# Dilated prompt heads by residue mod 4, diagonal tiles only, and the first blocks' row work in another order

## What is computed

```python
DSA_PAIRS = ((128, 1), (512, 4), (2048, 16))       # window, dilation; 2 heads each
def dsa_group_prompt(q, k, v, bias_tab, win, dil):
    '''Query t reads t - dil*j, j = 0..win/dil. ...'''
    ...
    s = jnp.where(valid[None, :, None, None], s + bias, -jnp.inf)
    p, lse = softmax_lse(s)
    o = jnp.einsum('bnrhqk,bnkrhd->bnqrhd', p, vv)...
    return o, lse
def dsa_combine(outs, lses):
    alpha = jax.nn.softmax(jnp.stack(lses, axis=0), axis=0)
    return jnp.concatenate([o * alpha[g][..., None] for g, o in enumerate(outs)], axis=2)
```

## Time and profile before

| | |
|---|---|
| median of 3 runs | 1014.61 us (1014.31 to 1015.29) |
| the profiled execution | 1012.51 us, span 1010.6 us |
| PE busy | 985.0 us, 97% of the span, 7695 matmul records |
| DVE busy | 495.5 us, 49% |
| ACT busy | 339.9 us, 34% |
| POOL busy | 67.3 us, 7% |
| share of PE on the chain that ended last | 90% |
| granted TensorE clock over the span | 0.998 |

### The profile page before, as it was taken

How to read it: one execution, slowest core, us unless ns; L and a number is a source line. 1 busy time by engine, 2 the same in 40 slices (tenths; PEclk the granted TensorE clock), 3 DMA queues, 4 the chain that set the end, 5 groups by cost and what they waited for, 6 DMA issues and landing times.

```text
span 1010.6 us, 18503 instructions
## 1 busy us (share of the span) xinstructions
PE 985.0 (97%) x7695; PEld 956.8 (95%) x7695; DVE 495.5 (49%) x906; ACT 339.9 (34%) x567; POOL 67.3 (7%) x91
## 2 busy tenths in 40 slices
PE   5899999999999999999999999999999999999997
PEld 5799989998998889899999999999999999999997
DVE  5634556655687313353535555554455544333232
ACT  6334233443455342322222343222222222322122
POOL 0100113011100200020204000000000000000000
PEclk9999999999999999999999999999999999999999
DMA  7586336332021564422331223222222223222202
GB/s 247 149 278 182 70 119 123 124 97 74 24 85 42 149 180 147 125 84 85 95 101 55 89 100 105 84 84 85 84 84 84 84 92 99 93 74 74 96 21 89
DMA packets 104605, 104.98 MB, mean 104 GB/s; under 512 B 10766, under 2 KB 101320, under 8 KB 104188
## 3 DMA queue, kind: packets, MB, share of 16 engines
q1 hardware_dynamic: 101224, 92.78, 30.2%
q0 software_dynamic: 3248, 11.03, 3.5%
q10 hardware_dynamic: 52, 0.01, 0.0%
HBM read 97.98 MB, written 14.89 MB: 112 GB/s over the span
## 4 chain that ended last, share of the span: by engine, by line
PE 90%; DVE 4%; DMA 1%; issue 1%; POOL 1%; ACT 1%; SPq 1%; ACTq 0%; DVEq 0%; POOLq 0%
PE acc L440 75%; PE acc L936 3%; PE acc L916 2%; PE acc L999 2%; PE acc L1035 1%; PE acc L926 1%; POOL mt L763 1%; PE acc L982 1%; PE acc L844 1%; PE acc L833 1%; SPq L641 1%; DVE h_lo L1883 1%; PE acc L804 1%; DMA ring<-in_cache_dsa_kv 1%; DVE w_lo L424 0%
## 5 line engine op out<-in xcount | busy, mean ns | idle before, releaser
L440 PE MATMUL acc<-h_hi,w_hi 128*128 128x256 f32 (+1 forms) x1520 | 471.7, 310 | 6.8 <-DVE w_lo L424 3.6
L440 PE MATMUL acc<-h_lo,w_hi 128*128 128x256 f32 (+1 forms) x1520 | 438.1, 288 | 0.0
L440 PE MATMUL acc<-h_hi,w_lo 128*128 128x256 f32 (+1 forms) x1520 | 436.7, 287 | 0.0
L440 PEld LDWEIGHTS acc<-h_hi,w_hi 128*128 128x128 f32 x1520 | 286.5, 188 | 16.7 <-issue 8.5
L440 PEld LDWEIGHTS acc<-h_lo,w_hi 128*128 128x128 f32 x1520 | 286.8, 189 | 6.5 <-issue 3.4
L419 ACT ACTIVATE w_hi<-raw 128x1024 fp32r<-128x1024 f32 x135 | 141.4, 1047 | 437.3 <-PE acc L440 437.2
L440 PEld LDWEIGHTS acc<-h_hi,w_lo 128*128 128x128 f32 x1520 | 286.7, 189 | 0.0
L424 DVE TENSOR_TENSOR w_lo<-raw,w_hi 128x1024 fp32r<-128x1024 f32 x135 | 165.4, 1225 | 111.4 <-ACT w_hi L419 106.8
L440 PE MATMUL acc<-s_hi,w_hi 128*128 128x256 f32 (+1 forms) x352 | 101.6, 288 | 0.0
L440 PE MATMUL acc<-s_lo,w_hi 128*128 128x256 f32 (+1 forms) x352 | 101.3, 288 | 0.0
L440 PE MATMUL acc<-s_hi,w_lo 128*128 128x256 f32 (+1 forms) x352 | 100.7, 286 | 0.0
(11 more groups left out here) (299 smaller groups left out, 1146.3 us busy)
## 6 DMA issues: line engine op xcount, KB each, us to landing
raw<-in_w_in SPq DMA_DIRECT2D x25, 1024.0 KB, 5.5
raw<-in_w_gate_up SPq DMA_DIRECT2D x22, 1024.0 KB, 4.9
raw<-in_w_down SPq DMA_DIRECT2D x8, 1024.0 KB, 5.3
ring<-in_cache_dsa_kv SPq DMA_DIRECT2D x4, 1024.0 KB, 6.8
raw<-in_w_out SPq DMA_DIRECT2D x4, 1024.0 KB, 5.6
out<-in_cache_dsa_kv SPq DMA_DIRECT2D x2, 2016.0 KB
rev<-tab POOLq DMA_DIRECT2D x1, 3840.0 KB, 15.9
ring<-in_cache_moba_k SPq DMA_DIRECT2D x48, 64.0 KB, 2.3
```

The lines of the kernel that those rows point to most:

```text
L440: ins = nc.tensor.matmul(acc[:, bank, 0:HALF[half]], a[:, k, :], two(b[:, kx + k, :], half), start=first and k == k0 and c == 0, stop=last ...
```

## The change

The prompt tokens of the far heads' q, k and v are stored in the order of their residue mod 4 when they leave PSUM, so that a query block of 128 positions holds one residue and needs just the one key tile with the same residue. A unit is now either near (`u` even: the near heads of both j) or far (`u` odd: four far heads, one tile each), still 8 units, one per block from block 18. Near and far parts have their own maxima and sums (`stat`), the probabilities are not normalised before the transposes, and at the end `factors` brings the parts to one softmax: the statistics are transposed on PE, stored to HBM and read back in both orders by POOL's DMAs, made into factors by DVE and ACT, sent through HBM again to all partitions, and DVE multiplies the outputs. Where branch B is handed on (`y_made`) the far heads are read back in their old order with a stride. In the first blocks `split_lo(1)` comes before `x_kept(6)` and `x_kept(7)`, and the row work is spread over blocks 1 to 4 and its PE part goes to block 5. SP's transfers beside (`gd`, `G`, the cache copies) move to later times with it.

```diff
+        def strided(ap):
+            return ap.rearrange("p (a j) -> p j a", a=NT)
+        def far(name, i):
+            return name in ("qb", "kb", "vb") and i > 0
+        ND = 2 * NT
+        units = [(i, [h]) for i in range(NT) for j in range(2) for h in range(6 + j, HEADS, 2)]
...
+        T_SA, T_F = 33, 29.55
...
+            t = t[:, n, 0:T if n < 2 else TP]
+            return t.rearrange("p (j a) -> p j a", a=NT) if n in (3, 4) else t
+        def y_made(n):
+            return strided(qT[:, n, 0:TP]) if n in (3, 4) else y_part(qT, n)
...
@@ SP
-                    yield 3.3
+                    yield 4.3
                     sp.wait_ge(sem("rows_done"), 1)
-                    yield 4
+                    yield 5
-                        yield 4 + g
+                        yield 6 + g
...
@@ POOL
+                def factors():
+                    pool.wait_ge(sem("st_ev"), 1)
+                    pool.dma_start(X["st"].rearrange("o (r p) -> (o r) p", p=P), st_T[:, :]).then_inc(sem("f_moved"), 16)
+                    pool.wait_ge(sem("f_moved"), 16)
+                    for s in range(2):
...
+                    pool.wait_ge(sem("f_dve"), 2)
+                    pool.dma_start(X["F"].rearrange("o (k r t) -> (o r) k t", k=2, t=P), F_exp[:, :, :]).then_inc(sem("f_moved"), 16)
+                    pool.wait_ge(sem("f_moved"), 16 * 8)
...
-                pool.wait_ge(sem("s_used"), ND * 3)
+                factors()
+                pool.wait_ge(sem("f_dve"), 4)
                 set_to(Qpad[:, :, :, :], 0.0, "qpad")
...
@@ PE
-                    yield 1.5
+                    yield 1.3
...
-                    yield 3.45
+                    yield 5.3
                     pe.wait_ge(sem("rows_done"), 2)
...
+                def dilated():
+                    for u in range(ND + 1):
...
+                            for j in range(2):
+                                if near(u):
+                                    ins = nc.tensor.matmul(out[:, j, :], zp[:, j, c:c + P], kT[:, 2, P * (i + 1 - keys_of(u)):P * (i + 1)],
+                                                           start=True, stop=True)
+                                else:
+                                    for g in range(2):
+                                        ins = nc.tensor.matmul(out[:, j, P * g:P * (g + 1)], zp[:, j, c + P * g:c + P * (g + 1)],
+                                                               kT[:, 3 + g, P * i:P * (i + 1)], start=True, stop=True)
...
@@ DVE
+                        if far(name, i):
+                            n = 2 * P
+                            if half == 1:
+                                v.then(scaled(dst[:, TP:T], src[:, n:n + TS], r[:, n:n + TS]))
+                            dst = strided(dst[:, 0:TP])[:, n // NT * half:n // NT * (half + 1), :]
+                            scaled(dst, src[:, 0:n].rearrange("p (j a) -> p j a", a=NT),
+                                   r[:, 0:n].rearrange("p (j a) -> p j a", a=NT)).then_inc(acc_ev, 1)
...
                 def factors():
...
+                    yield T_F
+                    dve.wait_ge(sem("f_moved"), 16 * 7)
...
+                    yield T_F + 0.6
+                    dve.wait_ge(sem("st_ev"), 2)
...
+                    yield T_F + 2.55
+                    dve.wait_ge(sem("f_moved"), 16 * 10)
...
                 x_lo(1)
+                split_lo(dve, 1)
                 x_kept(6)
                 x_kept(7)
```

More of the change, by code:

```diff
@@ L534, in unit_time, with near, keys_of, pair_view @@
         def unit_time(u, part):
[L536 removed]
+            return T_BLK + (u + part) / 4
         def scores_in(u):
[L540 removed]
+            return Sc[:, (ND + u) % 5, 0:widths[u]]
         def bias_of(h, c0, w):
[L543 removed]
+            return TTc[:, h - 6, c0:c0 + w]
+        def near(u):
+            return u % 2 == 0
+        def keys_of(u):
+            return min(u // 2, 1) + 1 if near(u) else 2
+        def pair_view(t, u):
+            w = P * keys_of(u)
+            return t.rearrange("p (j n) -> p j n", j=2)[:, :, 0:w]
+        def stat_of(s, u):
+            return stat[:, s, u % 2, :, u // 2]
         NC4 = (1, 2, 2, 2, 2, 2)
@@ L1067, in _ @@
                 x_turned(3, range(KD))
-                side = Side(rstd_rows(), bias_rows(), turn(), mlstm(), attention(), sample(), sample_outputs(), second_norm())
+                side = Side(rstd_rows(), bias_rows(), turn(), mlstm(), dilated(), attention(), sample(), sample_outputs(), second_norm())
                 def first_tile(half, k):
@@ L1223, in exps, with dilated, queries_of @@
                                          accum_out=dn[:, u % 4:u % 4 + 1]).then_inc(sem("e_done"), 1)
+                def dilated():
+                    def queries_of(u):
+                        act.wait_ge(sem("a_s"), HA * NT)
+                        if u == 0:
+                            act.wait_ge(acc_ev, sum_at[12])
+                        if u >= 2:
+                            act.wait_ge(sem("s_mm"), u - 1)
+                        i, c = u // 2, 2 * P * (u % 2)
+                        for j in range(2):
+                            p = HD * j
+                            if near(u):
+                                ins = nc.scalar.copy(zp[p:p + HD, j, c:c + P], qT[p:p + HD, 2, P * i:P * (i + 1)])
+                            else:
+                                ins = nc.scalar.copy(zp[p:p + HD, j, c:c + 2 * P].rearrange("p (g n) -> p g n", g=2),
+                                                     qT[p:p + HD, 3:5, P * i:P * (i + 1)])
+                            ins.then_inc(sem("zp_in"), 1)
+                    yield T_DIL - 0.3
+                    queries_of(0)
+                    for u in range(ND + 1):
+                        if u >= 1:
+                            yield T_DIL + u + 9 / 16
+                            act.wait_ge(sem("pt_tr"), u)
+                            if u >= 3:
+                                act.wait_ge(sem("o_mm"), u - 2)
+                            w = 2 * P * keys_of(u - 1)
+                            nc.scalar.copy(PTs[:, (u - 1) % 2, 0:w], acc[:, 6, 0:w]).then_inc(sem("pt_ev"), 1)
+                        if u < ND:
+                            yield T_DIL + u + 10 / 16
+                            act.wait_ge(sem("m_done"), u + 1)
+                            view = pair_view(Sc[:, u % 5, :], u)
+                            for j in range(2):
+                                nc.scalar.activation(view[:, j, :], view[:, j, :], ACT.Exp, bias=stat_of(0, u)[:, j:j + 1],
+                                                     accum_out=stat_of(1, u)[:, j:j + 1]).then_inc(sem("e_done"), 1)
+                        if u + 1 < ND:
+                            yield T_DIL + u + 13 / 16
+                            queries_of(u + 1)
+                    yield T_DIL + ND + 15 / 16
+                    act.wait_ge(sem("st_tr"), 1)
+                    nc.scalar.copy(st_T[:, :], acc[0:32, 6, 0:P]).then_inc(sem("st_ev"), 1)
+                    yield T_F + 0.4
+                    act.wait_ge(sem("f_dve"), 1)
+                    nc.scalar.activation(F_exp[:, :, :], F_exp[:, :, :], ACT.Exp).then_inc(sem("st_ev"), 1)
@@ L1388, in _ @@
                 x_hi(1)
-                side = Side(rstd_rows(), turn(), mlstm(), attention(), gates(), sample(), sample_softmax(), merge(), feed())
+                side = Side(rstd_rows(), turn(), mlstm(), dilated(), attention(), gates(), sample(), sample_softmax(), merge(), feed())
                 for w in range(n_all):
```

351 lines of the change are left out of this document (211 added, 140 removed).

## The result

The changed kernel takes 1000.6 us (median of four runs, 999.4 to 1002.8) against 1014.5 before: a ratio of 0.987, 95% interval 0.985 to 0.988. Forecast were 996.0 us and a range of 992.5 to 1000.5. The profiled execution took 1001.37 us, its span is 999.6.

A forecast was written before the change was run, and what follows sets the result against it. PE was taken to bound the kernel. Tiles removed (13.3 us) and first blocks reordered (5.3 us) summed to 18.6 us, taking 1014.6 to 996.0 us at chance 0.70; range 992.5 to 1000.5 us.

The forecast's parts named there:

- What bounds the kernel: Whole kernel: PE, busy 985.0 of 1010.6 us; a change pays where it takes work from PE or ends its waits.
- Term 1: Blocks 18 to 26: 24 dilated tiles removed, each with score, transpose and output; net 13.3 us, bounds 12.5 and 14.1.
- Term 2: First blocks: the new order ends PE's waits and the slow clock before block 3; net 5.3 us, bounds 3.5 and 6.4.
- The new waits: First blocks: second sum of block 2 read late, 0.2 us; turn of ka in block 4 waits, 0.9 us.
- Rival A: First blocks exchange one wait for another, 3 us or more, slow clock behind; only 1.9 us stay: 999.4 us, chance 0.12.
- (a): SP's transfers: `gd` about 1 us later, G wanted at block 7's start with 2 us margin; costed at nothing.
- (b): `factors` near block 29: DMAs land with 4 us margin, DVE's own 4 us fit its spare time; costed at nothing.
- D: DVE stands in `factors` until POOL's DMAs land, PE behind it; a loss of 20 us: 1016 us, chance 0.02.
- (c): Handing on of branch B: three pieces take 1.56 us on DVE, two now strided; costed at nothing.
- rival B: Strided elements double an operation; sums hide it, handing on of branch B loses up to 2.1 us: 998.1 us, chance 0.10.
- C: Dilated units bound by the round trip, PE waiting 0.9 us in each of 8; 7 us lost: 1003 us, chance 0.05.

The follow-up runs named there:

- e5: The changed kernel without the five small DVE operations of the second piece of `factors` and without the two multiplications by the factors: 995.5 us.
- e10: The changed kernel with the second piece of `factors`, its five operations together, moved three rows later: 1001.8 us.
- e9: The changed kernel itself, run again unchanged beside other experiments on one chip: 1000.5 us.
- e7: The changed kernel with the far heads handed on by residue, not turned back, so those rows reach the wrong tokens: 1000.4 us.
- e8: The changed kernel, same results, with DVE's `factors` work cut into seven pieces from block 28 and far factors stored by residue: 997.8 us.
- e11: e8 with POOL's clearing of `Qpad` also put behind the last scores: 997.7 us.
- e13: e11 with the pieces of `factors` whole again (2.4 and 2.05 us), in the same early blocks: 998.5 us.
- e6: The changed kernel with POOL's clearing of `Qpad` moved behind the wait for the last scores: 1000.6 us.
- e14: e11 with POOL's broadcast of the bias rows held until G has landed, and its wait put behind the state stores: 997.5 us.
- e1: The kernel before with only the new order of the first blocks: 1009.5 us, against 1013.9 for the kernel before on that chip.
- e12: e11 with each of the seven pieces of `factors` three units later: 997.2 us.

## Why the prediction was right or wrong

- **What bounds the kernel: right.** e5 shows it: take the waits away and the tiles' time comes out in full.
- **Term 1: right in kind, 0.6 us too small.** 13.9 us by PE's starts (14.4 by `w_lo` from 17 to 29), against 13.3 and a best bound of 14.1. (The bound was added up wrong: half of the 0.8 us of waits was in the 13.3 already, so with all of them gone it is 13.7, and the low end of the range 992.9.) The prices of a score, transposes and outputs stand unchanged in the chain after:

```profile
201.56 0.86 PE acc L986 x4
...
204.63 0.44 PE acc L1002 x4
...
207.48 0.89 PE acc L1014 x8
```

  Block 26's second sum starts at 244.39, 74.3 us behind block 17's (170.12); I had forecast about 74.8. So all of the 0.8 us of small waits went, where I had counted on half. What the table shows beyond it up to `w_lo` 29 is for the most part the late `w_lo` of the kernel before.
- **Term 2: 4.2 in the first profile and e10's, 4.8 to 6.0 in the others, against 5.3.** Some 1.7 us of it is the clock before, which was low from 40 to 50 us, where I had 1.3. Block 3 needs no wait; it starts at 37.11 in e9, where I had 37.2 (38.34 in the first profile):

```profile
36.46 1.23 DVE L435 TENSOR_TENSOR w_lo<-raw,w_hi 128x1024 fp32r<-128x1024 f32 x1 [2.86 <-ACT w_hi L430]
...
41.66 0.40 PE L451 MATMUL acc<-h_hi,w_hi 128*128 128x288 f32 x1 [0.33 <-DVE qT L1572]
...
47.48 0.66 PE L868 MATMUL acc<-con,kT 128*128 128x128 f32 x4 [0.58 <-DVE kT L1571]
```

  The new waits are the two that I had named, 0.3 and 0.6 us for 0.2 and 0.9. Rival A is refuted. What the first profile lacks is one run's: see the last section.
- **(a) SP and G at nothing: a small miss.** "its margin is 2 us" took G's landing from the kernel before, where the broadcast was issued 8 us ahead of G. After, three small DMAs of POOL and their landing (one before) move the broadcast back, and G goes out with it. The timelines of POOL and SP before, then after:

```profile
43.46 0.58 POOL L705 DMA_DIRECT2D rev<-tab  x1 [1.78 <-DMA tab<-tab]
...
51.56 0.35 SPq L608 DMA_DIRECT2D G<-gd  x1
```
```profile
47.55 0.55 POOL L748 DMA_DIRECT2D rev<-tab  x1 [3.89 <-DMA tab<-tab]
...
48.44 0.34 SPq L648 DMA_DIRECT2D G<-gd  x1
```

  Depending on the run that costs nothing or, as `w_lo` shows in e7, e8, e10, e11 and e13, 0.6 to 1.7 us.
- **(b) `factors` at nothing: the step that failed.** The DMA half of it held. They landed in time and DVE never waited for them, which refutes D. But "DVE's own 4 us lie in a stretch where it is busy for 52.48 of 66.20 us" took idle time for cover. Before, from `w_lo` 29 to 34, DVE's idle times there are mostly under 1 us, the longest 1.58, between a maximum, an exponential and a sum, each in order behind the other; 2.45 or 2.7 us in one go fit into none. The work was also sized too small: its three pieces are 5.9 us, not 4. Measured, the second and third piece cost 5.3 us (e5). Not all of that is their own length: of the changed kernel's loss 1.1 us goes away when only POOL's clearing moves (e6), another thing that I had at nothing, so the two overlap. This step makes the miss: without it the gain is 18.75 us; in the first profile term 1 was 0.6 us too small and term 2 1.1 too large, which by luck nearly cancel.
- **(c) strided accesses at nothing: wrong by 0.8 us**, the mechanism of rival B, at 0.8 instead of 2.1. Its sign, sums over 0.42 us, is there too (groups by shape; busy time and mean ns; before, then after, where by the mean four of the eight have strides; the last row is one of them):

```profile
L1438 DVE TENSOR_TENSOR kT<-acc,rstd 128x256 f32<-128x256 f32 x6 | 2.5, 413 | 0.0
```
```profile
L1572 DVE TENSOR_TENSOR kT<-acc,rstd 128x256 f32<-128x256 f32 x8 | 4.1, 511 | 2.0 <-PE acc L451 2.0
...
134.63 0.61 DVE L1572 TENSOR_TENSOR kT<-acc,rstd 128x256 f32<-128x256 f32 x1
```

  A strided sum takes 0.61, a plain one 0.41; PE's next user comes late enough to hide it. L1926 takes 2.04 us for 1024 elements, where e8's plain ones take 0.68 for 512: 1.5 times as long. The rule of the Trainium skill, "SBUF — State Buffer", "Door 1: The DMA port swizzle", that a cross to a new line of 16 bytes pays a penalty, thus speaks of a cost that these rows bear out; the Trainium skill gives no size, and the rows have half as much again where rival B had twice. L1926 reads its factors with a step of exactly 4 values, so that step is not free here either; the sums write with a step of 128.
- **C: refuted where I put it** (no wait for PTs from 174 to 245 us), but it is what happened in the MoBA units once DVE was late.

By the first profile: 14.4 + 4.2 - 6.0 - 0.8 + 0.4 (small waits in the sample part that went) = 12.2, with the 0.5 us of the late `w_lo` 29 in both the first and the third number.

## What to carry to other kernels

A share of busy time says how much work fits, not what size of piece. Before costing an addition at nothing on an engine that is 80% busy, look for its longest idle time there and for who stands in order behind it; then cut the addition to that size. (In these profiles cut pieces in earlier blocks lost 1.9 us instead of 6.0; what the size and the place each did is not separated.) And when a change moves the issue of a transfer, check which large one now goes out beside it.

## What the runs showed of the hardware

**After the same idle time the clock falls in one execution and not in another.** My term 2 counted the low clock behind the idle time before block 3 as a cost that the change ends. There it did end: all 14 profiles with the new first blocks show 1.00 from 30 to 50 us. But other places have it in some executions. In e8 and e14 PE stands still at the same place of the sample part, at 411 to 413 and 410 to 412 us; windows of e8, then of e14:

```profile
411.00:413.00 2.00, 0.41 (x3) 0.34 (x3) 2.00 (x5) 1.35 (x3) 0.00 (x0) 1.00 0.00 0
413.00:415.00 2.00, 2.00 (x11) 2.00 (x10) 2.00 (x4) 0.30 (x1) 0.00 (x0) 0.50 0.00 0
```
```profile
410.00:412.00 2.00, 0.42 (x5) 0.21 (x3) 2.00 (x5) 1.35 (x3) 0.00 (x0) 1.00 0.00 0
412.00:414.00 2.00, 2.00 (x16) 2.00 (x17) 2.00 (x4) 0.59 (x1) 0.00 (x0) 1.00 0.00 0
```

Behind the same wait of 1.58 us for a sum of DVE, with the same matmuls around it, the granted clock falls to 1.2 GHz in one and stays at 2.4 in the other. The two kernels differ in POOL's clearing and broadcast; what decides it, no run shows. In the table a fall cost 1.5 us (e6, e8 and e11, from 40 on) to about 1.6 us (e1, before 40, less its longer wait). Another place for it is at 980 to 995 us, in most profiles; e12's has none at all and gains 15.0 us in the span. The spread of the runs of one kernel, some 4 us, fits with this: the kernel before, beside e1, took 1014.2 to 1016.0 us in runs with a clock of 0.995 over the span and 1012.3 to 1014.0 with 0.998.

**The first products can run at about half speed where the window shows a full granted clock.** After, then e9, the same matmuls:

```profile
17.78 0.41 PE L451 MATMUL acc<-h_hi,w_hi 128*128 128x256 f32 x1
18.42 0.41 PE L451 MATMUL acc<-h_hi,w_hi 128*128 128x256 f32 x1
```
```profile
17.45 0.28 PE L451 MATMUL acc<-h_hi,w_hi 128*128 128x256 f32 x1
17.81 0.28 PE L451 MATMUL acc<-h_hi,w_hi 128*128 128x256 f32 x1
```

Three products take 0.64 us in the one, until 19.5 us, and 0.36 in the other, while both windows show 1.00, here after:

```profile
17.00:19.00 2.00, 2.00 (x11) 2.00 (x11) 2.00 (x6) 2.00 (x7) 0.00 (x0) 1.00 1.09 382
```

A step of 0.21 us is also what products of this shape take in e8 at 414 us, in the window with the clock at 0.50. So the array may have run at its lower level here too, with the window not showing it; no run decides that. This is the 1.2 us that the first profile lacks in the early blocks (e10's has it too), and it is of the run, not of the kernel.
